# A two-layer macaron block in fp32: the first panels of three FFNs read the unnormalized x, and the order of VectorE's work is changed

## The reference

```python
def rms_norm(x, g):
    y = x32 * lax.rsqrt(jnp.mean(x32 * x32, axis=-1, keepdims=True) + EPS)
    return y.astype(x.dtype) * g
def modulate(x, g, shift, scale):
    return rms_norm(x, g) * (1.0 + scale) + shift
def swiglu(h, w_in, w_out):
    g, u = jnp.split(h @ w_in, 2, axis=-1)
    return (jax.nn.silu(g) * u) @ w_out
def macaron_layer(x, mod, norm_g, w_in, w_out, mixer):
    m = [mod[:, :, i] for i in range(N_MOD)]
    x = x + m[2] * (0.5 * swiglu(modulate(x, norm_g[0], m[0], m[1]), w_in[0], w_out[0]))
    out, aux = mixer(modulate(x, norm_g[1], m[3], m[4]))
    x = x + m[5] * out
    x = x + m[8] * (0.5 * swiglu(modulate(x, norm_g[2], m[6], m[7]), w_in[1], w_out[1]))
```

## Time and profile before

| | us |
|---|---|
| median of 3 runs | 1729.56 |
| lowest, highest | 1726.78, 1731.93 |
| the profiled execution, its own time | 1733.21 |
| its span, first to last instruction | 1730.9 |
| TensorE busy in it | 1573.2 |
| VectorE busy in it | 1127.0 |
| mean granted TensorE clock | 0.956 of full |

### The profile page before, as it was taken

One profiled execution on the slowest core, in us unless ns is written; L12 is line 12 of the kernel. 1 busy time (PEld: TensorE's weight loads), 2 busy tenths in 40 slices (PEclk: granted clock), 3 DMA queues, 4 the chain that ended last, 5 costly groups with the idle time before them and its releaser, 6 DMA issues.

```text
span 1730.9 us, 21369 instructions
## 1 busy us (share of the span) xinstructions
PE 1573.2 (91%) x8665; PEld 1490.4 (86%) x8665; DVE 1127.0 (65%) x1827; ACT 614.8 (36%) x870; POOL 38.6 (2%) x46
## 2 busy tenths in 40 slices
PE   2699999889878799999979999988887997999999
PEld 2699999868657699999979999986775787999999
DVE  5897887768684587667867666785575745433432
ACT  2133332243363333332233333223336534333321
POOL 0000000000022000000000000000200000000000
PEclk9899999989988899999989999998898998999999
DMA  9165556523300355545625544551230011433333
GB/s 384 62 236 225 219 208 222 191 98 122 122 1 25 146 196 210 197 173 205 230 103 225 190 183 182 211 191 43 74 122 25 1 49 66 150 126 122 112 121 120
DMA packets 51569, 254.68 MB, mean 147 GB/s; under 512 B 6288, under 2 KB 8464, under 8 KB 36624
## 3 DMA queue, kind: packets, MB, share of 16 engines
q1 hardware_dynamic: 48896, 250.11, 39.3%
q10 hardware_dynamic: 2576, 3.22, 0.6%
HBM read 250.53 MB, written 2.77 MB: 146 GB/s over the span
## 4 chain that ended last, share of the span: by engine, by line
PE 74%; issue 14%; DVE 6%; DMA 2%; ACT 2%; POOL 1%; SPq 0%; POOLq 0%; DVEq 0%; ACTq 0%
PE ps L1289 24%; PE ps L1291 24%; PE ps L1290 24%; DVE mod_prod L787 1%; DVE w_lo L773 1%; DMA w_raw<-in_w_in 1%; DMA x<-in_xT 1%; ACT w_hi L484 1%; PE ps L1299 1%; DMA w_raw<-in_w_qkv 1%; DVE mx L1025 1%; POOL h_lo L470 1%; PE ps L1309 0%; DVE wm_first L787 0%; PE ps L1461 0%
## 5 line engine op out<-in xcount | busy, mean ns | idle before, releaser
L773 DVE TENSOR_TENSOR w_lo<-w_raw,w_hi 128x2048 fp32r<-128x2048 f32 (+2 forms) x186 | 376.2, 2023 | 382.8 <-ACT w_hi L484 381.5
L1289 PE MATMUL ps<-h_hi,w_hi 128*128 128x384 f32 x1536 | 521.0, 339 | 35.8 <-DVE w_lo L773 22.0
L1290 PE MATMUL ps<-h_lo,w_hi 128*128 128x384 f32 x1536 | 518.7, 338 | 0.0
L1291 PE MATMUL ps<-h_hi,w_lo 128*128 128x384 f32 x1536 | 518.5, 338 | 0.0
L484 ACT ACTIVATE w_hi<-w_raw 128x2048 fp32r<-128x2048 f32 (+2 forms) x186 | 315.7, 1697 | 375.0 <-DMA w_raw<-in_w_out 153.4
L1289 PEld LDWEIGHTS ps<-h_hi,w_hi 128*128 128x128 f32 x1536 | 293.0, 191 | 39.1 <-issue 16.1
L1290 PEld LDWEIGHTS ps<-h_lo,w_hi 128*128 128x128 f32 x1536 | 293.0, 191 | 0.0
L1291 PEld LDWEIGHTS ps<-h_hi,w_lo 128*128 128x128 f32 x1536 | 292.6, 190 | 0.0
L1291 PE MATMUL ps<-g_hi,w_lo 128*128 128x384 f32 x704 | 235.9, 335 | 0.0
L1290 PE MATMUL ps<-g_lo,w_hi 128*128 128x384 f32 x704 | 235.8, 335 | 0.0
L1289 PE MATMUL ps<-g_hi,w_hi 128*128 128x384 f32 x704 | 235.8, 335 | 0.0
(11 more groups left out here) (187 smaller groups left out, 1289.2 us busy)
## 6 DMA issues: line engine op xcount, KB each, us to landing
w_raw<-in_w_in SPq DMA_DIRECT2D x88, 1024.0 KB, 4.8
wm<-in_w_mod SPq DMA_DIRECT2D x128, 512.0 KB, 5.7
w_raw<-in_w_out SPq DMA_DIRECT2D x64, 704.0 KB, 4.1
w_raw<-in_w_qkv SPq DMA_DIRECT2D x12, 1024.0 KB, 4.8
wm_first<-in_w_mod SPq DMA_DIRECT2D x16, 512.0 KB, 17.6
w_raw<-in_w_o SPq DMA_DIRECT2D x8, 1024.0 KB, 4.8
w_raw<-in_w_qup SPq DMA_DIRECT2D x8, 576.0 KB, 3.6
w_raw<-in_w_down SPq DMA_DIRECT2D x4, 1024.0 KB, 4.8
```

What stands on the lines that cost most here:

```text
L773: nc.vector.tensor_tensor(w_lo[:, slot, 0:width], w_raw[:, slot, 0:width], w_hi[:, slot, 0:width].bitcast(F32), ALU.subtract).then_inc(w_l ...
L1289: nc.tensor.matmul(out, l_hi, r_hi, start=first, stop=False)
L1290: nc.tensor.matmul(out, l_hi, r_lo, start=False, stop=False)
L1291: return nc.tensor.matmul(out, l_lo, r_hi, start=False, stop=last)
```

## The change

In FFN 2, 3 and 4 (norms 2, 3, 5, called `DEFER`) the first two input panels no longer read the normalized activations. They read `xg`, x times the modulation's gain, which ScalarE and VectorE make block by block during the output projection ahead of it (`xg_high`, `xg_low`). The root of a token is a factor of its whole column, so it is applied when the result leaves PSUM (`scale_out`). The shift cannot be treated so: it rides along as two extra columns (`T + 2` = 386 columns), and its product with the weights is added behind the root. The sum of squares (TensorE) stands behind 6 of the 8 blocks of the first panel, the broadcast behind the first block of the second. The normalized activations are made meanwhile (`late_norm`) in three buffers `hn`, and panels 2 to 21 read them as before. For this the context tokens' modulation moves to ScalarE (`contexts`, like `latents`, with 128 columns), ScalarE copies the broadcast root from PSUM into `sqacc`, and the sum and the root use PSUM bank 6 instead of 6 and 4; panel m's banks become (0, 4, 2)[m % 3] for (0, 2, 4)[m % 3]. For norm 3 `xg` shares the buffer with the normalized activations, so ScalarE waits for TensorE block by block (`xg_used`).

In all stages the updates of x now stand ahead of the weight subtractions, and the last `high` and `low` of a stage behind its last square. The gains of the next norm are made at the start of the output projection. The modulation's units are dealt out anew, and `WM_SLOTS` is 5.

```diff
-WM_SLOTS = 6
+WM_SLOTS = 5
 def mod_units(name, f, m):
     if name == "in":
-        return {0: 3, 1: 3 if m < 6 else 2, 2: 2, 3: 0}[f]
-    return 2 if f < 3 else 0
+        return {0: 3, 1: 3 if m > 2 else 0, 2: 3 if m > 2 else 0, 3: 0}[f]
+    return {0: 2, 1: 1, 2: 2 if m < 14 else 0, 3: 0}[f]
...
+            def xg_high(n, k):
+                act.wait_ge(shift_ready, 2 * DEFER[n] + 1)
+                for s, seg in SEGS:
+                    ins = nc.scalar.activation(xg_of(n)[0][:, k, seg], x[:, k, seg], ACT.Copy, scale=gmul[:, k, s:s + 1])
+                ins.then_inc(xg_hi_done, 1)
+            def late_norm(f, n, layer, part):
+                shift = 72 * layer + 24 * part
+                base = PHASE["in", f][0]
+                high(base + 2)
+                act.wait_ge(bc_ready, n + 1)
+                nc.scalar.activation(sqacc[:], ps[:, 6, 0:T], ACT.Copy).then_inc(rb_ready, 1)
+                for k in range(KD):
+                    latents(n, k, gmul[:, k, 1:2], modc[:, shift + k, 1:2])
+                    contexts(n, k, gmul[:, k, 0:1], modc[:, shift + k, 0:1])
+                    if n == 3:
+                        if k < KD - 1:
+                            act.wait_ge(xg_used, k + 1)
+                        else:
+                            act.wait_ge(panel_used, base + 2)
+                    h_high(n, k)
+                    if k == 5:
+                        high(base + 3)
+                for m in range(2):
+                    act.wait_ge(scaled_out, 2 * DEFER[n] + m + 1)
+                    for s, seg in SEGS:
+                        ins = nc.scalar.activation(sg[:, m, seg], sg[:, m, seg], ACT.Silu, bias=wshift[:, m, s:s + 1])
+                    ins.then_inc(silu_done, 1)
+                for m in range(2):
+                    act.wait_ge(prod_ready, KF * f + m + 1)
+                    nc.scalar.activation(g_hi[:, m, :], prod[:, m, :], ACT.Copy).then_inc(g_hi_done, 1)
...
+            def ffn_out(f, late=None):
                 base = PHASE["out", f][0]
                 for j in range(2 * KD):
-                    if base + j + 2 < PANELS:
+                    if base + j + 2 < PANELS and j < 2 * KD - 1:
                         high(base + j + 2)
                     if j % 2 and f < 3:
                         squares(RES_BASE["out", f], j // 2)
-            def wo(l):
+                        if late:
+                            xg_high(late, j // 2)
+                if base + 2 * KD + 1 < PANELS:
+                    high(base + 2 * KD + 1)
+            def wo(l, late):
                 base = PHASE["wo", l][0]
                 for j in range(4):
-                    if j:
+                    if 0 < j < 3:
                         high(base + j + 2)
                     for k in (2 * j, 2 * j + 1):
                         squares(RES_BASE["wo", l], k)
+                        xg_high(late, k)
+                        if k == 6:
+                            high(base + j + 2)
...
+                if n in DEFER:
...
+            def shift_columns(n, layer, part):
+                shift = 72 * layer + 24 * part
+                hi, lo = xg_of(n)
+                nc.vector.tensor_copy(hi[:, :, T:T + 2], modc[:, shift:shift + KD, :]).then_inc(shift_ready, 1)
+                v.wait_ge(shift_ready, 2 * DEFER[n] + 1)
+                nc.vector.tensor_tensor(lo[:, :, T:T + 2], modc[:, shift:shift + KD, :],
+                                        hi[:, :, T:T + 2].bitcast(F32), ALU.subtract).then_inc(shift_ready, 1)
+            def xg_low(n, k):
+                hi, lo = xg_of(n)
+                v.wait_ge(xg_hi_done, xg_val(n, k))
+                for s, seg in SEGS:
+                    ins = nc.vector.scalar_tensor_tensor(lo[:, k, seg], x[:, k, seg], gmul[:, k, s:s + 1],
+                                                         hi[:, k, seg].bitcast(F32), ALU.mult, ALU.subtract)
+                ins.then_inc(xg_lo_done, 1)
+            def scale_out(f, n, m):
+                bank = bank_pair(m)
+                v.wait_ge(panel_used, PHASE["in", f][0] + m + 1)
+                for half in range(2):
+                    nc.vector.tensor_copy(wshift[:, m, 2 * half:2 * half + 2], ps[:, bank + half, T:T + 2])
+                nc.vector.tensor_tensor(sg[:, m, :], ps[:, bank, 0:T], sqacc[:], ALU.mult)
+                nc.vector.tensor_tensor(prod[:, m, :], ps[:, bank + 1, 0:T], sqacc[:], ALU.mult).then_inc(scaled_out, 1)
+            def late_norm(f, n, layer, part):
+                base = PHASE["in", f][0]
+                low(base + 2)
+                invert(n)
+                for k in range(KD):
+                    scaled(n, k)
+                    if k:
+                        h_low(n, k - 1)
+                    if k == 3:
+                        scale_out(f, n, 0)
+                h_low(n, KD - 1)
+                scale_out(f, n, 1)
+                low(base + 3)
+                for m in range(2):
+                    v.wait_ge(silu_done, KF * f + m + 1)
+                    for s, seg in SEGS:
+                        ins = nc.vector.scalar_tensor_tensor(prod[:, m, seg], prod[:, m, seg],
+                                                             wshift[:, m, 2 + s:3 + s], sg[:, m, seg],
+                                                             ALU.add, ALU.mult)
+                    ins.then_inc(prod_ready, 1)
+                for m in range(2):
+                    v.wait_ge(g_hi_done, KF * f + m + 1)
+                    nc.vector.tensor_tensor(g_lo[:, m, :], prod[:, m, :], g_hi[:, m, :].bitcast(F32),
+                                            ALU.subtract).then_inc(g_ready, 1)
...
-            def ffn_out(f, layer, part, after):
+            def ffn_out(f, layer, part, after, late=None):
                 base, rb = PHASE["out", f][0], RES_BASE["out", f]
                 for j in range(2 * KD):
                     k = j // 2
-                    if base + j + 2 < PANELS:
-                        low(base + j + 2)
                     mod_units_now(mod_units("out", f, j))
                     if j == 0:
                         residual_gains(layer, part, 0.5)
+                        if after:
+                            norm_gains(*after)
+                        if late:
+                            shift_columns(late, *after)
+                    if j % 2 == 0 and after:
+                        if k > 1:
+                            add_square(rb, k - 1)
+                        if late and k:
+                            xg_low(late, k - 1)
                     if j % 2:
-                        if after and k > 1:
-                            add_square(rb, k - 1)
-                        if after and k == KD - 1:
-                            norm_gains(*after)
                         v.wait_ge(panel_used, base + j + 1)
                         update(k, 6 + k % 2)
+                    if base + j + 2 < PANELS and j < 2 * KD - 1:
+                        low(base + j + 2)
                 if after:
                     add_square(rb, KD - 1)
-            def wo(l, after):
+                if late:
+                    xg_low(late, KD - 1)
+                if base + 2 * KD + 1 < PANELS:
+                    low(base + 2 * KD + 1)
+            def wo(l, after, late):
                 base, rb = PHASE["wo", l][0], RES_BASE["wo", l]
                 residual_gains(l, 1, 1.0)
+                norm_gains(*after)
+                shift_columns(late, *after)
                 for j in range(4):
-                    if j:
-                        low(base + j + 2)
-                    if j == 3:
-                        norm_gains(*after)
                     for b in range(2):
                         k = 2 * j + b
                         if k > 1:
                             add_square(rb, k - 1)
+                        if k:
+                            xg_low(late, k - 1)
                         if j % 2 and b == 0:
                             v.wait_ge(out_ready, 2 * l + j // 2 + 1)
                         else:
                             v.wait_ge(panel_used, base + j + 1)
                         update(k, (2 if j % 2 else 4) + b)
+                    if 0 < j < 3:
+                        low(base + j + 2)
                 add_square(rb, KD - 1)
+                xg_low(late, KD - 1)
+                low(base + 5)
...
+                def early(m, k):
+                    hi, lo = xg_of(n)
+                    for half in range(2):
+                        mm = mm3(ps[:, bank_pair(m) + half, 0:T + 2], *w_tile((base + m) % SLOTS, KD * half + k),
+                                 hi[:, k, 0:T + 2], lo[:, k, 0:T + 2], k == 0, k == KD - 1)
+                    return mm
+                if n in DEFER:
+                    pe.wait_ge(w_lo_done, base + 1)
+                    for k in range(KD - 1):
+                        if k == KD - 2:
+                            sum_squares(n)
+                        pe.wait_ge(xg_lo_done, xg_val(n, k))
```

(80 more changed lines are left out.)

64 lines of the change are left out of this document (38 added, 26 removed).

## The result

The changed kernel takes 1701.3 us (median of 4, 1699.74 to 1703.12) against 1730.7 for the kernel before beside it: ratio 0.983, 95% interval 0.981 to 0.986. The forecast was 1690, and 1683 to 1697 for the case thought likeliest; the range to 1705 holds the result, near its slow end. The profiled execution took 1703.12 (span 1701.1) where that of before took 1733.2: of the 40.0 us in the sum, 30.1 came.

What follows compares the result with a forecast made beforehand. TensorE was busy 1573 of 1731 us, so gains lay in its idle and slow stretches. 31.4 (three deferred FFNs) plus 8.6 (norms 1 and 4) made 40.0; 1729.6-40.0 = 1689.6, forecast as 1690, range 1678 to 1705.

Steps and rivals of the forecast that it cites:

- Norms 1 and 4: New order alone, counted from E, where TensorE's idle time before the sum begins: variance 4.3 us earlier, twice, 8.6.
- The sum: Ahead of each deferred FFN, the sum of squares on TensorE, inside panel 0, was to cost 0.7 us.
- root's wait: Before the broadcast in each deferred FFN, TensorE was to wait 1.1 us, with low(base+2) ahead of the variance on VectorE.
- the wait before panel 3: In each deferred FFN, TensorE was to wait 2.4 us for low(base+3), behind scale_out of panel 1 on VectorE.
- The broadcast: Broadcast of the root on TensorE, behind panel 1's first block in each deferred FFN: 0.75 us.
- Blocks 6 and 7: In panel 2, TensorE was to lose 1.05 us at block 7, as scale_out of panel 0 delays block 4's scaling.
- rival E: Matmuls of 386 columns might stream at a lower rate; 288 of them pay, 1840 at a quarter rate; chance 0.04.
- B: Ahead of the FFNs, ScalarE's and VectorE's chains take 1.8 a block instead of 1.45: 3 to 4 us each, 1701; chance 0.2.
- C: TensorE almost never waits: FFNs lose only sum and broadcast, 1676; a clock holding at norms 1 and 4 would add; chance 0.1.
- D: In FFN 3, VectorE falls late with the modulation's units and sets the pace: 10 to 15 us, 1703; chance 0.05.
- Two columns more cost what 128 more do in proportion: Matmuls of 386 columns in panels 0 and 1: 0.8 ns more each, 0.24 us for all 288.
- The clock should hold, since no stretch without matmuls is over 2.5 us: In the three deferred FFNs, TensorE's clock was to stay up through the short waits, so no clock loss was counted.

Runs made afterwards that it cites:

- experiment 1: The changed kernel with the normalized activations read at a row distance of 384 words again, only xg at 388: 1698.3 us, ratio 0.982 to the kernel before.
- experiment 5: The kernel of experiment 1 with hx_hi, hx_lo and the weight buffers each starting at a multiple of 512 bytes: 1690.9 us, ratio 0.979 to the kernel before.
- experiment 2 (`before_stride`): The kernel before with only the row distance of the normalized activations changed, 388 words instead of 384: 1743.6 us, ratio 1.008.
- experiment 6: The kernel before with unused bytes around h_lo, so that the low part alone starts 128 bytes off a multiple of 512: 1740.3 us.
- experiment 7: The kernel before with 256 unused bytes behind the low part, so that only the weight buffers are off a multiple of 512: 1729.8 us.
- experiment 8 (`before_both128`): The kernel before with unused bytes so that h_hi and h_lo both start 128 bytes behind a multiple of 512: 1748.1 us, ratio 1.010.
- `best`: Experiment 5's kernel with variance ahead of low(base+2), panel 1's scale_out and base+3's high and low earlier, last low behind variance at norms 1, 4: 1687.4 us.
- `best2_nowait`: Experiment 5's kernel with, at norms 2, 3 and 5, the variance ahead of low(base+2) and scale_out of panel 1 behind block 6: 1689.2 us, ratio 0.976.

## Why the prediction was right in sign and 11 us short

*Right, by its steps.* Norms 1 and 4: first matmul 10.7 after E (10.9 forecast, 15.2 before). The sum 0.73 (0.7), root's wait 0.93 to 1.02 (1.1), the wait before panel 3 1.95 (2.4), the pair of `xg_high` 0.387 and 0.495, near 0.8 with their overlap (0.85), a context 0.48 (0.48), a block of ScalarE's chain 1.50 (1.45). The broadcast was 0.93 (0.75). Blocks 6 and 7 cost 0.34 in two waits (0.48 in FFN 3) rather than 1.05. Matmuls of 386 columns start 0.1766 apart (0.174 forecast), 0.3 us for the 96 of one FFN: no rival E. Rivals B, C and D didn't happen: ScalarE's chain kept to 1.50 a block, not B's 1.8, so B's 1701 is met by chance; C's clock did not hold, and FFN 3 won its 7.5.

The Trainium skill, page "ScalarE: Activation LUTs", section "What ACT_TABLE_LOAD costs", states 93 ns a pointer operand, and the prediction's estimate from it put the pair near 0.8; the trace agrees.

*The term that was missing: where the buffers stand.* "Two columns more cost what 128 more do in proportion" was right of the matmul and blind to the buffer: 128 bytes more in `hx_hi` put `hx_lo` 128 bytes off. By the order of allocation `h_hi` and `h_lo` started at multiples of 512 bytes before, and after `hx_lo` at one plus 128. That costs 0.085 a panel, 7.5 us in 88 panels, and about 3 more in the 620 matmuls of 512 columns that read `hx` in attention; taking it away gave 1701.3-1690.9 = 10.4 (different chips; they are 29 and 39 below their own kernels before), or 7.4 by experiments 1 and 5. Experiments 2 and 5 to 8 show that the place of `h` sets the pitch of the matmuls that read it; by what mechanism is open.

*The step that failed: "The clock should hold, since no stretch without matmuls is over 2.5 us".* It fell behind a wait of 1.95, about 10 matmuls at 0.32 in place of 0.17: 1.5 us each FFN. The forecast's path was right up to there: in FFN 2 panel 3 started 30.9 after E (31.0 forecast) and ended at 40.9 (39.4). With both, the FFNs come out: 12.8, 10.9 and 7.7 were forecast, less 1.9 (22 panels) and 1.5 gives 9.4, 7.5 and 4.3; measured 9.6, 7.5 and 4.3. The match is closer than one run's noise warrants.

*The norms' 8.6.* The two attention stages gave 4.2 and 6.7, with the layout's loss in both. The surplus in attention 2 stands beside a clock of 0.96 against 0.93 in its 250 us. Attention has many short waits, and its granted clock differed by 0.1 among these kernels without a pattern that I could name; that part isn't explained.

*What the change consists of.* Order alone takes 1730.7 to 1708.8; deferral, with the buffers aligned, from there to 1690.9 (the new deal of units and the five held rows go with it; they were not run by themselves). Of the 49.7 us that the prediction read ahead of the FFNs 11.0 was VectorE's order, which it named as a gain for norms 1 and 4 only. That leaves its sum alone but changes the reason: deferral as timed, with its 10 us of layout, was worth 1708.8-1701.3 = 7.5.

## What to carry to other kernels

When a buffer grows by a few bytes, look at what starts behind it, and compare the pitch of matmuls in a stage that the change doesn't touch. Ahead of a small GpSimd operation on the critical path, keep VectorE's long operation back, even if that means a wait on VectorE. Try the new order of the queues by itself before a deeper change: it may hold most of the gain.

## What the runs showed of the hardware

- Matmuls of 384 fp32r columns on `h` start 0.1733 us apart when both its parts start at multiples of 512 bytes (eight kernels), 0.1751 or 0.1756 with the low part 128 bytes off (rows of 1552 and of 1536 bytes; five kernels), 0.1760 with both (one). With `h` as the operand held in the array and 512 columns of weights streaming it is 0.2267, 0.2311 or 0.2322, and 0.2324. Weights 256 off left both at 0.1733 and 0.2267 (one kernel). On `g`, at 192, 224 or 448 past a multiple, the pitch is 0.1733 in twelve kernels, but 0.1747 to 0.1767 in most FFNs of `before_stride` and `before_both128`, with `g` and the weights at the same starts. So a start is not the whole rule, and the rule is open.
- A root of 3 columns on GpSimd took 0.85 us without, and 2.83 beside, a 128x2048 subtraction on VectorE (all three late norms of `best` and `best2_nowait`). The Trainium skill, page "SBUF — State Buffer", section "Who interferes with whom", says that the two engines share a port; the trace agrees, and puts 2 us on a tiny operation.
- Behind a wait of 1.93 to 1.95 ahead of panel 3 the clock fell to half, for about 3 us, in seven of nine profiled FFNs; behind one of 0.86 to 0.89 at the same place it stayed at 1.00 in twelve of twelve.
